# Dilated heads: probabilities divided before the turn and streamed against value pairs on column halves

## The chip, the cores and the metric

One core of a Trainium2 chip runs the whole kernel in one launch. The metric is the device time in microseconds (us) of that core; the median of three runs of the kernel before is 2211.18 us (2210.8 to 2213.64).

## The reference, cut to what matters

The program is three transformer blocks on 512 tokens of width 1024, all in fp32: one block with two other attentions, and then two blocks ("layers" below) whose attention has 16 heads of width 64: four plain heads, four differential heads (two softmaxes each) and eight dilated heads. The change touches the eight dilated heads of both layers. Each dilated head combines three branches by their log-sum-exp, which is the same as one softmax over causal keys with the logarithm of a key's count added to its score:

```python
def dilated_attention(q, k, v, positions):
    ...
    for window, dil in DILATED_PATTERNS:
        o, lse = dilated_branch(q, k, v, window, dil)
        outs.append(o)
        lses.append(lse)
    wts = jax.nn.softmax(jnp.stack(lses, axis=0), axis=0)
    o = jnp.sum(wts[..., None] * jnp.stack(outs, axis=0), axis=0)
    return from_heads(o)
```

Behind it the 16 heads' outputs lie side by side (512 tokens x 1024) and are multiplied by `w_out`.

## The kernel before, in words

Tokens are kept in four tiles of 128. A layer's attention is a list of jobs, `two_jobs`: plain and differential heads alternate, and the eight dilated heads (L0 to L7 below) come last. Class `Plan` (from line 935) writes the order out by hand as steps. Each step has one score tile: 128 queries (tile j) against the 128(j+1) keys that are not in their future; within a dilated head j goes 3, 0, 2, 1. There are 80 score tiles, so steps 0 to 79; the dilated heads' are steps 48 to 79.

For one tile, `attend` does on four engines, in order:

- TensorE multiplies queries by keys into one of three score banks (line 1605); it may not run more than three scores ahead of VectorE's masks.
- VectorE adds the mask and finds the minimum (L2834, with a small read of the result), and ScalarE takes the exponential and the row sum (L2119).
- Three steps later TensorE turns the probabilities 128x128 by 128x128 (transposes, L1631) into one of two banks, and ScalarE copies them out (L2134); for j = 3 VectorE does (L2852).
- Another three steps later TensorE multiplies: a turned 128x128 block of probabilities is the loaded operand and 64 columns of values are streamed (L1617). A dilated head needs 1 + 2 + 3 + 4 = 10 such products. Output: 128 tokens x 64.
- When a head's four tiles are done, VectorE takes the reciprocals of the row sums (L2884) and scales the output into `O2` (`finish`, L2890).

In between, by step numbers in `O2_TURNS`, TensorE turns `O2` back, 128 columns (two heads) by four tiles at a time (`o2_transpose`, L1927), and ScalarE and VectorE split the turned tile into a high and a low part (`o2_high` L2592, `o2_low` L3516). The projection by `w_out` (`slab_features`, lines 1126 to 1128) then runs through four slabs of weights, two of these tiles each; the first slab needs the turned tiles 0 and 1, which are dilated heads 0 to 3. The eighth turned tile is made inside the first slab, behind its bank 2.

In the trace each fp32 matmul is two records, each with its own weight load; a transpose is one.

GpSimd splits weight slabs into high and low parts in slab order (L665, L669, function `run`), as each is loaded and its buffer is free; two of the four `w_out` slabs are split before the dilated heads begin, the third waits until TensorE has used the first.

The differential heads' outputs are normed by a chain at steps 58 to 64 (`DIFF_SQ`, `DIFF_SUM`, `DIFF_ROOT`, `DIFF_SCALE`): ScalarE squares, VectorE sums, ScalarE takes a root (with two table loads), VectorE scales (L2817, L2820). At the start of the attention of the first block, but not here, TensorE is given extra products (`release_clock`) to keep it busy.

Of the kernel before, what the change touches and what calls it, by code (L numbers as in the profile page):

```python
# [221 lines left out]
def build(nc, xT_d, slabs_d, ada_d, c_d, cols_d, rows_d, consts_d, strips_d, pos_d, cpos_d,  # L222
# [5 lines left out]
    with ctx:  # L228
# [140 lines left out]
        O2 = at("O2", 100352, [P, TT, D_MODEL])  # L369
# [4 lines left out]
        sq_2 = at("sq_2", 116736, [P, TT * 4 * HD])  # L374
# [65 lines left out]
        cmp_hidden, hidden_ready = sem("cmp_hidden"), sem("hidden_ready")  # L440
        hidden_turned, hid_copied = sem("hidden_turned"), sem("hid_copied")
        cmp_out, cmp_taken, ck_root, ck_ready = sem("cmp_out"), sem("cmp_taken"), sem("ck_root"), sem("ck_ready")
# [19 lines left out]
        scores_ready, scores_masked, probs_ready = sem("scores_ready"), sem("scores_masked"), sem("probs_ready")  # L462
        probsT_ready, copied_act, copied_dve = sem("probsT_ready"), sem("copied_act"), sem("copied_dve")
# [183 lines left out]

        @block.gpsimd
        def _(pool):
# [205 lines left out]
            def run(n0, n1):  # L855
# [3 lines left out]
                with pool.Fori(n0 // 2, n1 // 2) as i:  # L859
                    for s in (0, 1):  # L860
                        split(s, 2 * i + s, i)
# [5 lines left out]
            for n in [mlp0] + [mlp0 + N_UP + N_DOWN + layer * PER_LAYER + first for layer in range(LAYERS)  # L867
# [5 lines left out]
                for layer, ct in enumerate(COUNTS):  # L873
                    if n == INPUTS[layer].base:
                        at = input_low(INPUTS[layer])
                    if n == ct.up:
# [24 lines left out]


        class Place:


            def __init__(self):
                self.meets = self.slab = self.drain = self.norms = self.bank = 0
                self.tile = self.value = self.map = self.pair = self.acopies = self.dcopies = 0
                self.turn = self.turn_a = self.turn_d = self.part = self.ffn = self.conv = 0
                self.x = self.free = self.pairs = self.roots = self.mixes = self.folds = 0  # L910

        def meeting(name, eng, at_):

            def meet(n=1):
                for _ in range(n):
                    at_.meets += 1
                    eng.drain().then_inc(arrived[name], 1)
                    for other in ("pe", "act", "dve"):
                        eng.wait_ge(arrived[other], at_.meets)
            return meet  # L920

        def slab_view(t, slot, k, n):
            return t[:, slot, 0:k * n].rearrange("p (k n) -> p k n", k=k)

        TURN_LAG, PAIR_LAG, COMBINE_LAG = 3, 5, 2
        S_BANKS, PT_BANKS, O_BANKS = 4, 2, 2
        M_SLOTS, P_SLOTS, PT_SLOTS, P_PAIRS = 2, 4, 3, 8

        FILL = (1, 1, 1, 1, 1)
        FILL_2 = ()

        class Plan:


            def __init__(self, jobs):
                self.scores, self.values, self.sums = [], [], []
                for m, jb in enumerate(jobs):
                    self.sums.append([sum(len(x["q"]) for x in jobs[:m]) + c for c in range(len(jb["q"]))])  # L940
                tiles, m = [], 0
                while m < len(jobs):
                    group = [m + 1, m] if m + 1 < len(jobs) and is_pair(jobs[m + 1]) else [m]
                    for j in (3, 0, 2, 1):
                        for g in group:
# [2733 lines left out]
```

## Time and profile before

| what | value |
|---|---|
| runs | 2213.64, 2210.80, 2211.18 us (median 2211.18) |
| profiled execution, first to last instruction (span) | 2210.5 us |
| what lies around the span | 0.7 us to the median of the runs; the profiled execution has no other time of its own on the page |
| TensorE busy | 2158.2 us, 98% of the span |
| VectorE, ScalarE, GpSimd busy | 1498.9, 946.0, 1195.8 us |
| granted clock of TensorE, mean | 0.996 |

In the profile PE is TensorE's matmuls, PEld its weight loads, DVE VectorE, ACT ScalarE, POOL GpSimd. A record's duration contains its way through the array, so records of a busy PE overlap; what a record costs in a stream is the distance from its start to the next start. A granted clock of 1.0 is 2.4 GHz, of 0.5 is 1.2 GHz.

### The profile page before, as it was taken

Reading aid. Unit: us, or ns where it says so; the run is one execution under the profiler, and the core shown is the slowest. Engines: PE = TensorE matmul, PEld = TensorE weight load, DVE = VectorE, ACT = ScalarE, POOL = GpSimd, SP = SyncE. Lnnn points to the kernel's source line nnn. Section 1 sums busy time; section 2 is a strip of 40 time slices with the busy share of each in tenths; the row PEclk is TensorE's granted clock in tenths of the full one; section 3 lists DMA queues with packets and bytes.
Section 4 is the critical chain, followed back from the end, with each engine's and each line's share of the span. In section 5 each row is a group of like instructions: output and inputs, shape, how many; then the busy total and the mean of one; then the engine's idle time right before and its main releaser. Section 6 shows DMA issues by size and latency. Waiting matters only on the chain.

```text
span 2210.5 us, 33160 instructions
## 1 busy us (share of the span) xinstructions
PE 2158.2 (98%) x12377; PEld 1842.0 (83%) x12377; DVE 1498.9 (68%) x2234; ACT 946.0 (43%) x1891; POOL 1195.8 (54%) x594
## 2 busy tenths in 40 slices
PE   6999999999999999999999999999999999999997
PEld 4788888877899988887887898888897887889886
DVE  6834777554666592897646777677996727777676
ACT  3254663011556510544743555512545725455412
POOL 4747403776477677745016654577653037544675
PEclk9999999999999999999999999999999999999999
DMA  8322102522133233222002222322322002222221
GB/s 323 153 77 89 55 30 84 190 89 96 58 115 107 105 140 133 93 105 86 1 1 95 96 78 113 113 95 79 113 81 75 1 32 84 86 106 115 95 95 57
DMA packets 32776, 206.78 MB, mean 94 GB/s; under 512 B 4080, under 2 KB 4336, under 8 KB 11632
## 3 DMA queue, kind: packets, MB, share of 16 engines
q1 hardware_dynamic: 32192, 200.27, 24.8%
q10 hardware_dynamic: 432, 4.46, 0.5%
q8 instruction: 99, 1.62, 0.3%
q14 instruction: 53, 0.43, 0.1%
HBM read 202.61 MB, written 2.10 MB: 93 GB/s over the span
## 4 chain that ended last, share of the span: by engine, by line
PE 88%; DVE 6%; issue 1%; ACT 1%; DMA 1%; DVEq 1%; POOL 1%; POOLq 0%; SPq 0%; ACTq 0%
PE PS L1126 18%; PE PS L1128 18%; PE PS L1127 18%; PE PS L1605 5%; PE PS L1617 5%; PE PS L1382 3%; PE PS L1381 3%; PE PS L1383 3%; PE PS L1631 3%; PE PS L1457 2%; PE PS L1459 2%; PE PS L1458 2%; PE PS L1256 1%; PE PS L1259 1%; PE PS L1258 1%
## 5 line engine op out<-in xcount | busy, mean ns | idle before, releaser
L665 POOL TENSOR_TENSOR w_hi<-raw,zero_c 128x512 fp32r<-128x512 f32 (+1 forms) x135 | 281.6, 2104 | 545.5 <-PE PS L1128 544.3
L669 POOL TENSOR_TENSOR w_lo<-raw,w_hi 128x512 fp32r<-128x512 f32 (+1 forms) x135 | 365.0, 2723 | 5.8
L1126 PE MATMUL PS<-b_hi,w_hi 128*128 128x512 f32 x512 | 203.1, 397 | 0.9 <-POOL w_lo L888 0.9
L1127 PE MATMUL PS<-b_lo,w_hi 128*128 128x512 f32 x512 | 203.0, 396 | 0.0
L1128 PE MATMUL PS<-b_hi,w_lo 128*128 128x512 f32 x512 | 203.0, 396 | 0.0
L3345 DVE TENSOR_TENSOR b_lo<-a_all,b_hi 128x512 fp32r<-128x512 f32 x44 | 162.6, 3733 | 49.3 <-ACT b_hi L2490 49.3
L1126 PE MATMUL PS<-f_hi,w_hi 128*128 128x512 f32 x448 | 177.6, 397 | 0.7 <-DVE f_lo L2647 0.7
L1128 PE MATMUL PS<-f_hi,w_lo 128*128 128x512 f32 x448 | 177.6, 396 | 0.0
L1127 PE MATMUL PS<-f_lo,w_hi 128*128 128x512 f32 x448 | 177.6, 396 | 0.0
L688 POOL TENSOR_TENSOR w_lo<-raw,w_hi 128x512 fp32r<-128x512 f32 x48 | 70.9, 1477 | 92.9 <-ACT w_hi L2482 92.9
L1126 PEld LDWEIGHTS PS<-b_hi,w_hi 128*128 128x128 f32 x512 | 96.4, 188 | 24.6 <-POOL w_lo L888 1.1
L1128 PEld LDWEIGHTS PS<-b_hi,w_lo 128*128 128x128 f32 x512 | 96.4, 188 | 23.5
L1127 PEld LDWEIGHTS PS<-b_lo,w_hi 128*128 128x128 f32 x512 | 96.4, 188 | 23.5
L1617 PEld LDWEIGHTS PS<-z,ring 128*128 128x128 f32 x640 | 87.0, 191 | 25.7 <-issue 12.2
L1128 PEld LDWEIGHTS PS<-f_hi,w_lo 128*128 128x128 f32 x448 | 84.4, 188 | 20.5
L1126 PEld LDWEIGHTS PS<-f_hi,w_hi 128*128 128x128 f32 x448 | 84.4, 188 | 20.1 <-issue 1.0
L1127 PEld LDWEIGHTS PS<-f_lo,w_hi 128*128 128x128 f32 x448 | 84.4, 188 | 19.1
L2490 ACT ACTIVATE b_hi<-a_all 128x512 fp32r<-128x512 f32 x44 | 25.3, 623 | 171.4 <-PE PS L1128 171.4
L677 POOL TENSOR_TENSOR w_lo<-raw,w_hi 128x2048 fp32r<-128x2048 f32 (+1 forms) x18 | 59.0, 3293 | 62.2 <-ACT w_hi L2342 62.2
L773 POOL TENSOR_TENSOR w_lo<-raw,w_hi 128x512 fp32r<-128x512 f32 x54 | 71.4, 1323 | 38.4 <-ACT w_hi L2380 38.4
L3307 DVE SCALAR_TENSOR_TENSOR aux<-PS,cols,aux 128x511 f32<-128x511 f32 (+1 forms) x112 | 81.0, 741 | 14.7 <-ACT aux L2462 13.5
L1617 PE MATMUL PS<-z,ring 128*128 128x64 f32 x640 | 85.3, 266 | 1.4 <-ACT ring L2134 1.4
(586 smaller groups left out, 6868.7 us busy)
## 6 DMA issues: line engine op xcount, KB each, us to landing
raw<-slabs_dram SPq DMA_DIRECT2D x161, 1024.0 KB, 4.8
aux<-ada_dram SPq DMA_DIRECT2D x18, 512.0 KB, 5.7
ada_first<-ada_dram SPq DMA_DIRECT2D x11, 512.0 KB, 14.1
cmpw<-cmpw_dram ACTq DMA_DIRECT2D x2, 2048.0 KB, 12.7
ada_late<-ada_dram SPq DMA_DIRECT2D x8, 512.0 KB, 3.2
ada_last<-ada_dram SPq DMA_DIRECT2D x8, 512.0 KB, 6.4
xT<-xT_dram SPq DMA_DIRECT2D x1, 2048.0 KB, 9.3
out_dram<-t SPq DMA_DIRECT2D x4, 512.0 KB, 3.2
```

The source lines that it names most:

```text
L665: high = nc.gpsimd.tensor_tensor(w_hi[:, slot, c], raw[:, slot, c], zero[:, 0:c.stop - c.start], ALU.add)
L669: low = nc.gpsimd.tensor_tensor(w_lo[:, slot, c], raw[:, slot, c], w_hi[:, slot, c].bitcast(f32), ALU.subtract)
L688: return nc.gpsimd.tensor_tensor(pair_ring(w_lo, ct, n, what), pair_operand(ct, n, what), pair_ring(w_hi, ct, n, what).bitcast(f32), ALU.s ...
L773: nc.gpsimd.tensor_tensor(ring_slot(w_lo, j), operand(j), ring_slot(w_hi, j).bitcast(f32), ALU.subtract).then_inc(slab_split if name == "A ...
L1126: nc.tensor.matmul(out, a_hi_, b_hi_, start=start, stop=False)
L1127: nc.tensor.matmul(out, a_hi_, b_lo_, start=False, stop=False)
L1128: return nc.tensor.matmul(out, a_lo_, b_hi_, start=False, stop=stop)
L1381: nc.tensor.matmul(out, wh[:, k, :], xh, start=first, stop=False, skip_group_check=True)
L1605: nc.tensor.matmul(PS[:, step % s_banks, 0:128 * nb], query_tile(jobs[m]["q"][c], j), jobs[m]["k"][:, 128 * lo:128 * (lo + nb)], start=Tru ...
L1617: last = nc.tensor.matmul(PS[:, 6 + m % O_BANKS, 64 * j:64 * j + 64], turned_slot(ring, v, 512)[:, 128 * b:128 * b + 128], jobs[m]["v"](lo ...
L3307: V.scalar_tensor_tensor(out=t[:, sh:], in0=src[:, 0:SEQ - sh], scalar=cols[:, w:w + 1], in1=t[:, sh:], op0=ALU.mult, op1=ALU.add)
L3345: V.tensor_tensor(b_lo[:, f, :], a_all[:, f, :], b_hi[:, f, :].bitcast(f32), ALU.subtract).then_inc(b_low_ready, 1)
```

## The change

For the eight dilated heads ("wide" jobs) only:

- The row sum's reciprocal is taken tile by tile on VectorE, two steps behind the score (32 small instructions a layer), and GpSimd multiplies the probabilities by it in place (`normalise`, 32 instructions a layer). On GpSimd's queue this stands behind the first two `w_out` slabs and ahead of the third.
- The turn waits for GpSimd and comes five steps behind the score instead of three; six slots of probabilities instead of four. The copies out of the turn's banks go to a whole-head buffer `wide_pT` (four of them), not to the ring.
- When both heads of a pair are turned, `wide_values` multiplies: 64 columns of values are loaded, and the turned probabilities of one key block, 512, 384, 256 or 128 queries long, are streamed. Head 2i goes to output partitions 0 to 63 and head 2i+1 to 64 to 127 of one bank; the two alternate. The four pairs come at steps 62, 70, 78 and, for the last, inside the first `w_out` slab behind its bank 0.
- The result lies turned already, so `O2` keeps only the plain and differential heads, the dilated heads' `finish` and four of the eight `o2_transpose` go, and `o2_high`/`o2_low` read the pair's bank.
- The first `w_out` slab takes its banks in order 0 to 7; three semaphores of another stage become one; buffers move.

```diff
+        TURN_LAG, PAIR_LAG, COMBINE_LAG = 3, 5, 2
+        WIDE_LAG, WIDE_INV_LAG, WIDE_VALUE_LAG = 5, 2, 2
...
                 for t in tiles:
-                    due[t] = t[2] + TURN_LAG
+                    due[t] = t[2] + (TURN_LAG if jobs[t[0]]["wide"] is None else WIDE_LAG)
...
-                    self.pvs.setdefault(turn + 2, []).append(v)
-                    self.takes.setdefault(turn + 3, []).append(v)
-                self.steps = turn + 4
+                    if not self.is_wide[v]:
+                        self.pvs.setdefault(turn + 2, []).append(v)
+                        self.takes.setdefault(turn + 3, []).append(v)
+                self.steps = turn + (1 if self.is_wide[-1] else 4)
+                self.wide_step = {pair: at_step[vs[-1]] + WIDE_VALUE_LAG for pair, vs in self.pair_values.items()}
...
-        O2_TURNS = [(56, 4, 3), (59, 5, 7), (63, 0, 10), (67, 6, 8), (70, 7, 8), (73, 1, 12), (80, 2, 14)]
+        O2_TURNS = sorted([(56, 4, 3), (59, 5, 7), (67, 6, 8), (72, 7, 8)] + [(wide_at[pair], pair, None) for pair in range(4)])
...
+            def normalise(layer):
+                plan = Plan(two_jobs)
+                for w, i in enumerate(plan.wide_scores):
+                    m, _, j, _ = plan.scores[i]
+                    _, nb = key_range(two_jobs[m], j)
+                    probs = probs_slot((ring_2, ring_x, ring_y), plan.slots[i], 128 * nb)
+                    pool.wait_ge(wide_inv_ready, len(plan.wide_scores) * layer + w + 1)
+                    nc.gpsimd.tensor_scalar(probs, probs, wide_inv[:, w % 8:w % 8 + 1], None, ALU.mult
+                                            ).then_inc(wide_normed, 1)
...
                         if is_pair(jobs[m]):
                             pe.wait_ge(combined, joined[v])
+                        elif plan.is_wide[v]:
+                            pe.wait_ge(wide_normed, w0 + plan.wide_scores.index(i) + 1)
...
+            def wide_values(pair, copied):
+                for ready in (copied_act, copied_dve):
+                    pe.wait_ge(ready, max(count for s_, count in copied if s_ is ready))
+                for b in range(TT):
+                    for g in (0, 1):
+                        h = 2 * pair + g
+                        last = nc.tensor.matmul(PS[64 * g:64 * g + 64, 6 + pair % 2, 128 * b:512],
+                                                z2[:, 5, b, 64 * h:64 * h + 64], wide_pT[h % 4][:, b, 128 * b:512],
+                                                start=b == 0, stop=b == TT - 1, skip_group_check=True)
+                last.then_inc(turned, 1)
...
+                    if step - WIDE_INV_LAG in plan.wide_scores:
+                        i = step - WIDE_INV_LAG
+                        w, (m, _, j, _) = plan.wide_scores.index(i), plan.scores[i]
+                        dve.wait_ge(probs_ready, g0 + i + 1)
+                        if w >= 8:
+                            dve.wait_ge(wide_normed, at_.wide + w - 7)
+                        V.reciprocal(wide_inv[:, w % 8:w % 8 + 1], rowsum[:, plan.sums[m][0] % 8, j:j + 1]
+                                     ).then_inc(wide_inv_ready, 1)
...
                 def last_turn(b):
-                    if b == 2:
+                    if b == 0:
                         o2_transpose(KD - 1)
...
-                              bank_ready=o2_banks, order=(0, 1, 2, 4, 5, 6, 7, 3), after=last_turn)
+                              bank_ready=o2_banks, order=range(KD), after=last_turn)
```

## Rows read from the trace of the kernel before

**Rows 1.** The page, part 1: busy time and share of the span:

```profile
PE 2158.2 (98%) x12377; PEld 1842.0 (83%) x12377; DVE 1498.9 (68%) x2234; ACT 946.0 (43%) x1891; POOL 1195.8 (54%) x594
```

**Rows 2.** Windows: the dilated stretch of layer 1, of layer 2, layer 2's end:

```profile
core 0: us, PE busy (x) PEld busy (x) DVE busy (x) ACT busy (x) POOL busy (x), PEclk, DMA share, GB/s
1087.76:1139.63 51.87, 50.42 (x372) 43.27 (x371) 35.05 (x108) 36.17 (x108) 0.00 (x0) 1.00 0.01 1
1735.00:1787.00 52.00, 50.54 (x370) 43.29 (x370) 35.92 (x113) 36.85 (x112) 0.00 (x0) 1.00 0.00 1
1783.00:1789.00 6.00, 6.00 (x55) 5.95 (x55) 2.62 (x9) 3.30 (x10) 0.00 (x0) 1.00 0.00 0
```

**Rows 3.** Timeline of PE, head L3: start, length, line, records:

```profile
1105.54 1.02 PE L1605 MATMUL PS<-T2a,T 128*128 128x512 f32 x2
1106.40 0.78 PE L1617 MATMUL PS<-z,ring 128*128 128x64 f32 x6
...
1108.08 0.81 PE L1605 MATMUL PS<-T2a,T 128*128 128x384 f32 x2
1108.73 1.00 PE L1617 MATMUL PS<-z,ring 128*128 128x64 f32 x8
1109.57 0.39 PE L1631 MATMUL PS<-consts,ring 128*128 128x128 f32 x2
1109.80 0.60 PE L1605 MATMUL PS<-T2a,T 128*128 128x256 f32 x2
1110.23 0.33 PE L1617 MATMUL PS<-z,ring 128*128 128x64 f32 x2
1110.40 0.61 PE L1631 MATMUL PS<-consts,ring 128*128 128x128 f32 x4
1110.84 0.60 PE L1927 MATMUL PS<-consts,O 128*128 128x128 f32 x4
```

**Rows 4.** Groups of DVE and ACT in 1092 to 1132 us:

```profile
L2834 DVE CUSTOM_DVE_ANT_0 ring<-PS,strip 128x256 f32<-128x256 f32 x7 | 3.0, 423 | 3.9 <-PE PS L1605 3.9
L2852 DVE COPY ring<-PS 128x512 f32<-128x512 f32 x7 | 4.8, 691 | 3.4 <-PE PS L1617 1.7 <-PE PS L1631 1.7
L3516 DVE TENSOR_TENSOR o_lo<-PS,o_hi 128x512 fp32r<-128x512 f32 x6 | 4.1, 688 | 0.4 <-ACT o_hi L2592 0.2
L2884 DVE RECIPROCAL stats<-rowsum 128x4 f32<-128x4 f32 x7 | 1.2, 175 | 0.2
L2890 DVE TENSOR_TENSOR O<-PS,stats 128x256 f32<-128x256 f32 x7 | 3.0, 425 | 0.5
...
L2119 ACT ACTIVATE ring<-ring,negmax 128x256 f32<-128x256 f32 x7 | 3.5, 502 | 0.3 <-DVE negmax L2834 0.3
L2592 ACT ACTIVATE o_hi<-PS 128x512 fp32r<-128x512 f32 x6 | 3.5, 584 | 0.0
```

**Rows 5.** Groups of POOL, all of the span:

```profile
L665 POOL TENSOR_TENSOR w_hi<-raw,zero_c 128x224 fp32r<-128x224 f32 x2 | 1.1, 558 | 0.0
L786 POOL TENSOR_TENSOR w_hi<-raw,zero_c 128x512 fp32r<-128x512 f32 x8 | 8.2, 1041 | 21.9 <-DMA raw<-slabs_dram 21.7 <-issue 0.2
L783 POOL TENSOR_TENSOR w_lo<-raw,w_hi 128x512 fp32r<-128x512 f32 x8 | 10.3, 1290 | 0.4 <-issue 0.4
```

**Rows 6.** DVE with two operands in SBUF: POOL idle, and the page's:

```profile
L2820 DVE TENSOR_TENSOR O<-O,rows 128x1024 f32<-128x1024 f32 x1 | 1.2, 1226 | 0.1
...
L3345 DVE TENSOR_TENSOR b_lo<-a_all,b_hi 128x512 fp32r<-128x512 f32 x44 | 162.6, 3733 | 49.3 <-ACT b_hi L2490 49.3
```

**Rows 7.** Windows in the first block's attention:

```profile
225.00:228.00 3.00, 1.49 (x11) 1.36 (x12) 1.21 (x5) 2.97 (x9) 2.15 (x2) 1.00 0.00 0
228.00:231.00 3.00, 3.00 (x13) 2.40 (x12) 1.26 (x3) 1.59 (x6) 3.00 (x3) 0.50 0.01 3
```

More of the change, by code:

```diff
@@ L645, in _, with __init__ @@
             sp.wait_ge(stored, 16 * KD // 2)
+        class Place:
+            def __init__(self):
+                self.meets = self.slab = self.drain = self.norms = self.bank = 0
+                self.tile = self.value = self.map = self.pair = self.acopies = self.dcopies = 0
+                self.turn = self.turn_a = self.turn_d = self.part = self.ffn = self.conv = 0
+                self.x = self.free = self.pairs = self.roots = self.mixes = self.folds = 0
+                self.narrow = self.wide = 0
@@ new lines, in turned_slot, with on_vector, key_range, job @@
+        def turned_slot(ring, u, n):
+            return ring[0][:, M_SLOTS + P_SLOTS + u % PT_SLOTS, 0:n]
+        def on_vector(jb, j):
+            return j == TT - 1 and jb["vector"]
+        def key_range(job, j):
+            lo = max(0, j - 2) if job["window"] else 0
+            return lo, j - lo + 1
+        def job(q, k, v, out, strip=None, window=False, coef=None, mode="set", turned_by=None, vector=True, wide=None):
+            return dict(wide=wide, vector=vector, q=q if isinstance(q, tuple) else (q,), k=k, v=v, out=out, strip=strip, window=window, coef=coef, mode=mode, turned_by=turned_by)
@@ new lines, in apart, with laid, turned_counts @@
+        def apart(n, src, slots, masks):
+            parts = [(slots[i], masks[:, i:i + 1]) for i in range(masks.shape[1])]
+            return (src, P, parts, []) if n % 2 == 0 else (src, P, [], parts)
+        def laid(bank, dst):
+            return bank.rearrange("p (t d) -> p t d", t=TT) if len(dst.shape) == 3 else bank
+        def turned_counts(items):
+            out, a, d = [], 0, 0
+            for _, _, acts, dves in items:
+                a, d = a + len(acts), d + len(dves)
+                out.append((a, d))
+            return out
@@ new lines, in build, with turn_split @@
+        two_turns += [apart(i, two_src(3, 128 * i), dilated_q[2 * i:2 * i + 2], halves) for i in range(4)]
+        two_turns += [whole(i, two_src(4, 128 * i), P, T2a[:, i, :], 1.0) for i in range(4)]
+        two_turn_chunk = [2] * 2 + [0] * 2 + [1] * 2 + [0] * 2 + [3] * 4 + [4] * 4
+        HEAD = 8
+        turn_step = {step: HEAD + n for n, step in enumerate((3, 8, 13, 18, 23, 28, 33, 38))}
+        def turn_split(src, hi, lo, n, gains=None):
+            return [(lambda tt, i=i: src(tt, i), hi[:, i, :], lo[:, i, :], gains[i] if gains else None)
+                    for i in range(n)]
@@ L900, in _ @@
                     pool.drain()
[L903 to L920, printed above, removed]
@@ L1590, in attend @@
                         copies.append((copied_act, a))
+                return copies, a, d
+            def attend(jobs, ring, s_banks=S_BANKS, banks_ready=None, also=None, fill=FILL):
+                plan = Plan(jobs)
+                g0, v0, m0, p0 = at_.tile, at_.value, at_.map, at_.pair
+                w0 = at_.wide
+                (copies, a, d), joined = value_copies(jobs, plan), []
+                for m, j, _ in plan.values:
                     at_.pair += is_pair(jobs[m])
@@ L1940, in _ @@
                 at_.turn_d += KD
[L1941 removed]
+                order = o2_order
                 def o2_banks(b):
```

416 lines of the change are left out of this document (219 added, 197 removed).

## The prediction

> **What bounds the kernel now.** The page comes first: TensorE is busy 98% of the span [rows 1], so what ends last is its stream nearly everywhere, and an edit is worth what it takes out of that stream less the idle time it puts in. Next the windows: the stretch from the first dilated score to the first product of the projection lasts 51.9 us in layer 1 and 52.0 in layer 2, with TensorE idle 1.45 us in each, all at full clock; the last 6 us have no idle at all [rows 2]. VectorE and ScalarE are busy 35 and 36 us of the 52, GpSimd not at all. Then the timeline, where the price of a record is the distance to the next start [rows 3]: a score of 512, 384 or 256 columns costs 0.86, 0.65 or 0.43 us, so 0.22 for 128 and 2.16 for a head's four; eight records of the value product take 0.84 us (0.105 each), four of a transpose 0.44 (0.11). A value record streams 64 columns, by the score's rate 0.054 us: it costs twice that, as much as a transpose, so its 128-column load sets it.
>
> Sums go against the span of 2210.5 us; what lies around it (0.7 to the median) is left alone, so a difference is taken from the median, 2211.18. About 0.2%, 4.4 us, is what a measurement of this kernel tells from no change.
>
> **Part 1: TensorE's stream, per layer.** Removed: 8 heads x 10 products x 2 records x 0.105 = 16.8 us, and 4 x 4 turns of O2 x 0.11 = 1.8; together 18.6. Added: per pair 4 key blocks x 2 heads x 2 records, of 512, 384, 256 and 128 columns; loads of 64 columns hide behind streams at least that long. Nothing in this trace uses half of the array's columns, so the price is bounded. Above: every record at the score's price, 2 x 2.16 = 4.3 us a pair, 17.3 a layer, net 1.3 saved. Below: the heads of a pair wholly beside each other, 8.6, net 10.0 saved. They use different columns of the array and different output partitions and alternate in the code, so I take them to run side by side, but starting in order: a head's second record waits for its first, so the pair runs as nine slots, 3 x 0.43 + 2 x 0.325 + 2 x 0.215 + 2 x 0.11 = 2.6 us, 10.4 a layer, net **8.2 saved**. The nearest rows (whole-array records, never two at once [rows 3]) are the upper end; I set it apart as a rival.
>
> The Trainium skill, "TensorEngine Tiling (Array Packing)", Key Properties, states that tiles execute in parallel, but also that changing the tiling mode drains the engine; no run here shows either yet. By the first the stream is the 8.2 saved, by the whole-array rows 1.3.
>
> Going from whole to half columns and back happens eight times a layer. Bound: nothing, or the way through the array that a stream hides, 0.33 less two times 0.105, so 0.12 us [rows 3], 1.0 a layer. I take **0.6**.
>
> **Part 2: the last tile has no cover.** Before, value products fill TensorE while the last tiles are masked, exponentiated and turned, hence the full last 6 us. After, behind the last score (step 79) only 15 transposes remain, 1.65 us. The chain from that score, with rows' durations [rows 4]: mask 0.42, exponential 0.50 (1.0 with hand-overs); ScalarE copies a turned tile of 384 columns (about 0.4, an estimate from the 0.58 of a like operation over 512) and takes the high part of pair 2 (0.58): 2.0; VectorE, in order, takes that low part (0.69) ahead of the last reciprocal (0.18): 2.85; then it copies the turned 512-wide tile (0.69), whose bank the second last turn needs: 3.5; GpSimd divides meanwhile; the two last turns follow (0.55): 4.1. So 4.1 - 1.65 = **2.4 us idle** a layer (2.1 to 2.8). The last pair's product then comes behind bank 0, by when its copies are done, and its high and low parts (1.3 us) hide behind banks 1 to 6.
>
> **Part 3: the clock.** In the first block TensorE was busy 1.49 of 3.0 us and the next 3 us were granted 0.5 [rows 7]; it loses half of those, 1.5 us. The tail is busy 1.65 of 4.1. Nothing or 1.7 us; I take **1.0** a layer.
>
> **Part 4: GpSimd.** The dividing has one tensor and one number a row. Rows [rows 5]: 0.56 us for 224 columns and 1.04 for 512, where one operand is a repeated zero, so 1.68 ns a column and 0.18 fixed: 1280 columns and four instructions make 2.9 us a head. With two full operands (1.29 for 512) at most 3.5. TensorE's pace will be 2.16 + 1.1 (ten turns) + 1.3 = 4.5 a head, so GpSimd keeps up. On its queue the dividing stands behind two splits that end before the stretch (POOL is idle throughout it [rows 2]) and ahead of the third, which waits for TensorE's first slab as before: nothing. SP's queue is not passed by anything.
>
> Latency: a turn comes five steps behind its score, but the reciprocal sits behind the mask two steps on. For a 512-wide tile: 1.5 us to the third score's end, 0.7 to its mask's end, 0.18, then 1.04, 3.4 us with hand-overs; TensorE's five steps hold 3.7 without a product in them. The margin is 0.3, so some turns wait: nothing to 1.5, I take **0.4** a layer, since each pair's product lets the others catch up.
>
> **Part 5: VectorE and ScalarE.** VectorE loses eight finishes (0.175 + 0.425) and gains 32 reciprocals at no more than 0.175: 35.1 - 4.8 + 5.6 = 35.9 us; ScalarE stays at 36 [rows 2, 4]. TensorE's stream in the stretch falls to about 40. The cover over these two goes from 14 to 4 us, and their work is not even: until step 61 no product fills TensorE, while VectorE finishes the differential heads. There I put 1.0 us (0 to 2). Around steps 62 to 67 the norm of the differential heads blocks first ScalarE, then VectorE, and turned tile 6 waits for it; less of the product's stream covers it than before, and its two passes over 1024 columns read two operands in SBUF (1.23 us alone) while GpSimd now works; such an operation took 3.73 us for 512 columns where GpSimd was splitting weights [rows 6]. There 0.8 (0 to 2.5). Together **1.8**.
>
> On the last point the Trainium skill, "SBUF — State Buffer", section "SBUF: two separate sides", says that GpSimd and a VectorE instruction with two SBUF inputs lock each other out for a whole instruction. By it each pass waits for one division at most, which lies inside that bound.
>
> **Sum** per layer: -8.2 + 0.6 + 2.4 + 1.0 + 0.4 + 1.8 = -2.0, two layers -4.0: 2211.2 - 4.0 = **2207 us**. With every bound of parts 2 to 5 at its end: from 2199 (-8.2 + 2.1 = -6.1 a layer; 2195 with the lower end of part 1) to 2218 (-8.2 + 2.8 + 1.7 + 1.0 + 1.5 + 4.5 = 3.3). The other edits move buffers and semaphores, at nothing: each wait on the merged semaphore names the same event, and the slab's new bank order waits for tiles that are ready by then.
>
> **Rivals.**
> 1. *One half behind the other: slower.* If records on half the columns queue like the others, the stream saves 1.3, while the tail still costs 2.4, clock 1.0, mode 0.6. Longer products give the others more time, so waits are 1.2 in place of 2.2. Per layer +3.9: **2219**, 2213 to 2222. For it: every pair of matmul records in the trace follows one another. Against: disjoint columns and partitions. The point that decides is a pair's product at about 3.2 us (18.6 less what parts 2 to 5 cost, by four); above, no gain is left.
> 2. *Side by side, and the others keep up.* Only the tail and mode changes cost: -8.2 + 2.4 + 0.6 = -5.2 a layer: **2201**, 2196 to 2204. For it: VectorE and ScalarE are idle 16 us of the stretch now, much of it waiting for TensorE. Against: their work bunches at the norm.
> 3. *GpSimd sets the pace.* From 4.5 us a head on it decides; at twice the two-operand price, 7.0, it adds 20 us a layer less the waits it covers: about **2243**. Against: no row of POOL is near that price per column.
>
> The change could also fail to do what it says only by rival 1's route; the removed records are certain.
>
> **Chances.** Forecast 0.40, rival 1 0.33, rival 2 0.22, rival 3 0.05. Faster than 2206.8: 0.17 of the forecast's 0.40, since its number, 2207, stands on that bound (its own range is 2199 to 2218), and rival 2: 0.39. Within 0.2%: 0.19 of the forecast and 0.07 of rival 1: 0.26. Slower than 2215.6: 0.04 of the forecast, 0.26 of rival 1, rival 3: 0.35. The likeliest case gives 2207. Cases of both signs hold most of the chance, so the range runs from rival 2's end, 2196, to rival 1's, 2222; it leaves out rival 3 and the tails, under 2 in 10.
>
> **What would show it.** Part 1: the pair's products as 16 records with 64 loaded columns, 2.6 us from first to next start if side by side, 4.3 if not; whether two records of different halves start together. Part 2: idle of some 2.4 us between the last score and the first projection product, released by VectorE's copy or GpSimd. Part 3: a window at 0.5 behind it. Part 4: the new POOL group at about 1.0 us for 512 columns. Part 5: idle of TensorE before scores, released by the mask, at the norm's place. The prediction is wrong if the stretch changes by more than 8 us, or if TensorE waits for GpSimd at most turns.

## The result, and the profile after

The changed kernel takes 2219.89 us (median of 6 runs, 2218.94 to 2222.52) against 2212.11 for the kernel before on the same chip: ratio 1.0037, 95% interval 1.0026 to 1.0049. It is slower by 0.37%. The prediction said 2207 and faster; its range, to 2222, held the time. The profiled execution took 2222.52 us, the longest of the six, and its mean granted clock is the lowest, 0.993 against 0.995 and 0.996 in the other five, so what is read from it is at the upper end, the price of the clock above all. The page's first line, which answers to [rows 1]:

```profile
PE 2153.6 (97%) x12153; PEld 1815.0 (82%) x12153; DVE 1493.7 (67%) x2266; ACT 946.2 (43%) x1891; POOL 1267.8 (57%) x658
```

Windows of the changed kernel: the stretch from the first dilated score to the first product of the projection in layers 1 and 2, then two pieces of layer 1, behind the norm and behind the tail:

```profile
core 0: us, PE busy (x) PEld busy (x) DVE busy (x) ACT busy (x) POOL busy (x), PEclk, DMA share, GB/s
1085.66:1140.03 54.37, 44.80 (x248) 28.84 (x247) 33.41 (x126) 35.37 (x107) 34.41 (x32) 0.94 0.00 1
1740.91:1795.23 54.32, 44.75 (x249) 28.80 (x247) 33.56 (x126) 35.29 (x107) 34.40 (x32) 0.94 0.00 1
1112.50:1119.30 6.80, 6.00 (x18) 3.45 (x17) 3.97 (x13) 2.84 (x11) 3.07 (x3) 0.50 0.00 0
1139.80:1143.20 3.40, 3.40 (x11) 2.33 (x12) 0.00 (x0) 0.86 (x2) 0.00 (x0) 0.50 0.00 0
```

The same two stretches of the kernel before, here from the start of the first dilated score, as in the windows above ([rows 2] have layer 1's from a little earlier and a rounded window of layer 2):

```profile
1087.81:1139.63 51.82, 50.37 (x372) 43.22 (x371) 34.99 (x108) 36.12 (x108) 0.00 (x0) 1.00 0.01 1
1736.92:1788.74 51.82, 50.36 (x372) 43.22 (x371) 34.99 (x108) 36.13 (x108) 0.00 (x0) 1.00 0.00 1
```

From the start of one layer's stretch to the next it is 1740.91 - 1085.66 = 655.25 us, where before it was 1736.92 - 1087.81 = 649.11: 6.1 us a layer. The stretch was 51.82, with TensorE busy 50.37. Now it is 54.37, with TensorE busy 44.80, and idle 9.57 in place of 1.45. Of the busy time 3.0 us are the price of half clock: in the 6.8 us of the third window TensorE is busy 6.0, and a score of 512 columns takes 1.71 us to the next start there, where it took 0.86 [rows 3]. So the stretch is 5.57 + 3.0 = 8.6 us shorter in work, 8.1 longer in idle time, and 3.0 longer by the clock. Behind it stand the last pair's product (2.4), a turn of `O2` less (0.4), and another 3.4 us at half clock (fourth window, 1.7 lost). In all per layer: work -6.6, idle time +8.1, clock +4.7, sum +6.2, and 6.1 is what the starts show. (The spans differ by 10.2 us and not by two times 6.1, as the stretch of layer 1 starts 2.15 us earlier than before; its start lies anywhere from 1084.1 to 1088.7 us in the runs below.)

TensorE's timeline at the first pair's product (start, length, line, records; `128*64` is the loaded operand):

```profile
1104.96 0.30 PE L1681 MATMUL PS<-consts,ring 128*128 128x128 f32 x1 [0.16 <-ACT T L2206]
1105.19 0.64 PE L1700 MATMUL PS<-wide_pT,z 128*64 128x512 f32 x1
1105.20 0.64 PE L1700 MATMUL PS<-T,z 128*64 128x512 f32 x1
1105.67 0.59 PE L1700 MATMUL PS<-wide_pT,z 128*64 128x512 f32 x1
...
1107.29 0.27 PE L1700 MATMUL PS<-wide_pT,z 128*64 128x128 f32 x1
1107.49 0.70 PE L1653 MATMUL PS<-T2a,T 128*128 128x256 f32 x2
```

Two records of different heads start 10 ns apart: the halves work side by side. From the first start to the next score it is 2.30 us, where a pair's sixteen records would cost 4.3 at the price of records on the whole array [rows 3].

What TensorE's matmuls waited for in layer 1's stretch, and under it what its weight loads waited for (us in total, times, longest). No score (L1653) is among the matmuls that waited; all are turns, and what they waited for are copies and low parts:

```profile
PE PS L1681 <- ACT T L2206: 3.4, 4, 1.7
PE PS L1999 <- DVE o_lo L3608: 2.8, 2, 1.4
PE PS L1681 <- DVE wide_pT L2938: 1.6, 2, 0.8
PE PS L1681 <- ACT ring L2211: 1.2, 1, 1.2
```

```profile
PEld PS L1681 <- issue: 8.7, 14, 1.6
PEld PS L1681 <- POOL ring L1045: 4.8, 5, 1.8
PEld PS L1681 <- POOL ring_y L1045: 2.0, 3, 1.3
```

GpSimd's groups in the same stretch (count, busy us and mean ns, idle before):

```profile
L1045 POOL TENSOR_SCALAR ring<-ring,stats 128x512 f32<-128x512 f32 x5 | 7.8, 1565 | 52.1 <-DVE stats L2923 52.1
L1045 POOL TENSOR_SCALAR ring<-ring,stats 128x384 f32<-128x384 f32 x6 | 7.5, 1246 | 3.8 <-DVE stats L2923 3.8
L1045 POOL TENSOR_SCALAR ring<-ring,stats 128x256 f32<-128x256 f32 x6 | 5.5, 925 | 3.6 <-DVE stats L2923 3.6
L1045 POOL TENSOR_SCALAR ring<-ring,stats 128x128 f32<-128x128 f32 x5 | 3.0, 604 | 0.9 <-DVE stats L2923 0.9
```

A head's four divisions take 1.565 + 1.246 + 0.925 + 0.604 = 4.34 us. The two operands' rows [rows 5] had given at most 3.5.

VectorE and ScalarE beside the product of 1105.19 to 1107.49, and TensorE ahead of it and behind it:

```profile
1106.27 0.55 DVE L2912 CUSTOM_DVE_ANT_0 ring<-PS,strip 128x384 f32<-128x384 f32 x1
...
1108.23 0.42 DVE L2912 CUSTOM_DVE_ANT_0 ring<-PS,strip 128x256 f32<-128x256 f32 x1 [1.33 <-PE PS L1653]
```

```profile
1106.86 0.61 ACT L2191 ACTIVATE ring<-ring,negmax 128x384 f32<-128x384 f32 x1 [1.18 <-DVE negmax L2912]
...
1107.59 1.28 ACT L2678 ACT_TABLE_LOAD   x1
...
1109.37 1.28 ACT L2191 ACT_TABLE_LOAD   x1
```

```profile
1101.47 0.63 PE L1999 MATMUL PS<-consts,O 128*128 128x128 f32 x4 [1.39 <-DVE o_lo L3608]
...
1103.99 0.81 PE L1653 MATMUL PS<-T2a,T 128*128 128x384 f32 x2
...
1111.79 0.63 PE L1681 MATMUL PS<-consts,ring 128*128 128x128 f32 x4 [1.66 <-ACT T L2206]
...
1126.87 0.63 PE L1999 MATMUL PS<-consts,O 128*128 128x128 f32 x4 [1.43 <-DVE o_lo L3608]
```

While the product runs, TensorE makes no score, and VectorE runs dry for 1.33 us. ScalarE's 1.18 us are another matter: the score of 384 columns that it waits for was begun at 1103.99, ahead of the product, but VectorE, behind with the norm's sum, a copy and a low part, masked it at 1106.27 only. Behind the product both are late: ScalarE loads its tables for the norm's root and back, two times 1.28 us, with the copy behind them, and TensorE waits 1.66 us for that copy and is at half clock from 1112.5 on. The kernel before has the same two loads. VectorE's and ScalarE's busy time, 33.4 and 35.4 us, is no more than before [rows 2].

### The profile page after: what moved, and what is told of

Its sections match the earlier page's. It is cut to its first block, busy times and chain, and to the rows that moved or that the text cites. A ratio compares the mean times of both kernels' runs of the same rounds, so it can differ in the third digit from the quotient of the medians.

```text
span 2220.7 us, 32738 instructions
## 1 busy us (share of the span) xinstructions
PE 2153.6 (97%) x12153; PEld 1815.0 (82%) x12153; DVE 1493.7 (67%) x2266; ACT 946.2 (43%) x1891; POOL 1267.8 (57%) x658
## 4 chain that ended last, share of the span: by engine, by line
PE 83%; DVE 8%; issue 2%; DMA 2%; ACT 1%; DVEq 1%; POOL 1%; POOLq 1%; SPq 0%; ACTq 0%
PE PS L1167 18%; PE PS L1169 18%; PE PS L1168 18%; PE PS L1653 5%; PE PS L1665 3%; PE PS L1422 3%; PE PS L1424 3%; PE PS L1423 3%; PE PS L1681 2%; PE PS L1498 2%; PE PS L1500 2%; PE PS L1499 2%; DMA raw<-slabs_dram 1%; PE PS L1700 1%; DVE PS L3525 1%
## 5 line engine op out<-in xcount | busy, mean ns | idle before, releaser
L1045 POOL TENSOR_SCALAR ring<-ring,stats 128x384 f32<-128x384 f32 (+3 forms) x44 | 47.3, 1085 | 120.9 <-DVE stats L2923 120.9
L972 POOL TENSOR_TENSOR w_lo<-raw,w_hi 128x1024 fp32r<-128x1024 f32 x24 | 66.0, 2766 | 28.3 <-DVE aux L3535 20.2
```

## The experiments

All were timed in five rounds beside the kernel before; a ratio is to that kernel on the same chip, with its 95% interval. The changed kernel stands at 1.0037.

**1. The division left out.** The reciprocals stay, the division goes:

```diff
-                        normalise(layer)
...
-                            pe.wait_ge(wide_normed, w0 + plan.wide_scores.index(i) + 1)
+                            pe.wait_ge(probs_ready, g0 + i + 1)
...
```

> Leaves out the division of the dilated heads' probabilities (the reciprocals are still taken); a turn waits for the exponential itself. Theory (the chain through GpSimd sets TensorE's waits: TensorE's loads wait 6.8 us a layer for GpSimd's divisions, and idle time brings half clock): most of those waits go, the stretch from the first dilated score to the projection falls from 54.4 to about 49 to 50 us a layer and the time from 2220 to about 2210. Rival A (the work of VectorE and ScalarE, placed at fixed steps, sets the waits): the waits move to the masks and copies, at most 2 us gained, 2218. Rival B (half clock after the tail and the norm is the whole loss): 2217 to 2218, since both places of idle stay.

Measured: 2218.76 us, ratio 1.0031 (1.0022 to 1.0040). The first theory fell. The table of waits had put 6.8 us a layer on GpSimd; with GpSimd gone the same loads wait for the exponential, and the matmuls' waits stand where they were (stretch of layer 1, lines shifted by one):

```profile
PE PS L1680 <- ACT T L2205: 3.4, 4, 1.7
PE PS L1998 <- DVE o_lo L3605: 2.8, 2, 1.4
```

```profile
PEld PS L1680 <- ACT ring L2190: 8.1, 8, 1.8
PEld PS L1680 <- ACT ring_y L2190: 1.5, 2, 0.9
```

So a wait that stands on a weight load is not by itself a cost to the matmuls.

**2. One column divided.** `tensor_scalar` on `probs[:, 0:1]`, the hand-overs as they were.

> GpSimd divides one column in place of 128 to 512 (the rest of the division is left out), so that its two hand-overs stay and its 4.3 us a head shrink to an estimated 1.1 (4 x 0.28, the fixed part of the line through 0.604 and 1.565 us). Theory that the price per column was mis-sized: the time comes within 2 us of the kernel without the division. If the hand-overs from VectorE to GpSimd to TensorE cost as much as the work: half way between that kernel and the changed one, about 2215. Rivals A and B as there: 2217 to 2218.

Measured: 2217.80, 1.0031 (1.0022 to 1.0041), the same as without: neither GpSimd's work nor its hand-overs held most of the time.

**3. The heads one behind the other.** In `wide_values` the loop over the two heads goes outside the one over key blocks.

```diff
-                for b in range(TT):
-                    for g in (0, 1):
+                for g in (0, 1):
+                    for b in range(TT):
```

> The changed kernel, but a pair's product takes the four records of one head and then those of the other, in place of head by head in turn. Theory: the two heads then share nothing, the pair's product goes from 2.30 to about 4.3 us, and as other engines catch up meanwhile some of the 8 us a layer is covered: 5 to 7 us a layer more, 2230 to 2234. If the sharing is worth nothing here because TensorE waits anyway: 2220 to 2222.

Measured: 2236.12, 1.0110 (1.0095 to 1.0126). The first pair's product:

```profile
1105.56 1.93 PE L1700 MATMUL PS<-wide_pT,z 128*64 128x512 f32 x5
1107.12 0.64 PE L1700 MATMUL PS<-T,z 128*64 128x512 f32 x1
...
1108.02 1.46 PE L1700 MATMUL PS<-T,z 128*64 128x384 f32 x6
1109.41 0.70 PE L1653 MATMUL PS<-T2a,T 128*128 128x256 f32 x2
```

It takes 3.85 us in place of 2.30 (the last records of one head still run beside the first of the other). Four times 1.55 are 6.2 us a layer, and the time is 8.1 a layer longer. TensorE's idle time in the stretch is 10.7 us in its trace, where the changed kernel has 9.6: the longer product covered nothing. That speaks against any cover by the product.

**4. Waits for the own bank only, one turn later.**

```diff
-(59, 5, 7)
+(61, 5, 7)
...
-                    pe.wait_ge(turned_dve, base + n)
+                    pe.wait_ge(turned_dve, base + max([m + 1 for m in range(n) if O2_TURNS[m][1] >= 4], default=0))
```

> Turns of the differential tiles wait only for the earlier tile of their own PSUM bank (the third no longer for the low part of the second pair), and the second of them stands two steps later, 61 in place of 59. Theory: two waits of 1.4 us a layer go, 2.8 a layer, and half of it is taken up by the next wait: 2215 to 2217 (2214.3 if all of it stays). Rival A (other engines set the pace in this stretch): the wait appears at the next score or turn, 2219 to 2220.

Measured: 2219.11, 1.0035 (1.0021 to 1.0049). The two waits of 1.4 us for VectorE's low parts went and the next ones grew (1.72 us for ScalarE's copy, 1.97 for VectorE's behind the norm), as rival A had it.

**5. The products spread.** One key block a step, over four steps; own banks as in 4.

```diff
+        wide_block = {wide_at[pair] + b: (pair, b) for pair in range(3) for b in range(TT)}
...
+                    if step in wide_block:
+                        o2_transpose(o2_order.index(wide_block[step][0]), [wide_block[step][1]])
```

> The products of the first three pairs are taken one key block a step over four steps, in place of four blocks at one step; the differential tiles wait for their own bank only. After the first four runs the theory is: TensorE is idle 8.5 us a layer at fixed places, with or without the division, because a pair's product is one lump that covers nothing elsewhere, where before the value products lay evenly between the scores. By it the idle time falls to 3 to 5 us a layer, the stretch from 54.4 to about 49 to 50 us, and with a little for twelve more changes of mode a layer the time is 2210 to 2213. Rival C (VectorE's and ScalarE's work at the norm of the differential heads sets the waits, wherever the products lie): the waits before step 66 stay and 2217 to 2219 is measured.

Measured: 2214.77, 1.0014 (1.0005 to 1.0023). Three fifths of the loss go; no half clock is left in the stretch, 51.16 us long, and TensorE is idle 6.7 us of it in place of 9.6. The pieces cost more than the lump: 1.01, 0.79, 0.58 and 0.37 us from first start to next score, 2.75 against 2.30.

**6. The norm's passes left out.** VectorE's two passes that scale the differential heads are left out.

> Leaves out VectorE's two passes over the differential heads that apply the norm and its gain (2 x 1.23 us a layer); the squares, the sums and the root stay. Rival C (the norm sets the waits): the idle 1.66 and 0.80 us behind it and the 3.4 us lost at half clock after it go, 5 us a layer, 2210. The lump theory: the 2.5 us at most, part of it taken up by the waits next to it, 1 to 2.5 a layer, 2215 to 2218.

Measured: 2216.11, 1.0022 (1.0013 to 1.0031): 1.9 us a layer for 2.5 us of VectorE's work, and not all of what was lost. In its trace the wait of 0.80 us behind the passes goes and that of 1.66 stays; idle time falls by 0.5 us a layer only, and the time at half clock from 10.2 to 3.4 us.

**7. ScalarE's copies ahead of its exponential**, where a step turns dilated tiles alone: the loop over `plan.turns` moved up in ScalarE's `attend`.

> ScalarE copies the turned tile of a step ahead of that step's exponential in place of behind it. If TensorE's waits for ScalarE's copies (4.6 us in the stretch of layer 1: 3.4 for earlier copies' slots and banks and 1.2 for a differential one) come from the copy's place behind an exponential that waits for VectorE's mask, they go and some of the half clock with them: 3 to 5 us a layer, 2210 to 2214. If the copies are late because VectorE and ScalarE as a whole are late there, the wait turns up at the masks: 2218 to 2221.

Measured: 2215.81, 1.0022 (1.0013 to 1.0031), two fifths of what was lost, though nothing is computed less. Its trace does not show where the gain lies: in place of the waits of 1.66 and 0.80 us stand three of 0.56, 1.39 and 1.58, the idle time is 9.6 us a layer as in the changed kernel, and the half clock, 3.4 us a layer in place of 10.2, is that of one execution, for the runs' mean clocks (0.994 to 0.996) are no higher than the changed kernel's.

**8. The third pair's product two steps later**, `self.wide_step[2] += 2`.

> The third pair's product is taken two steps later, at step 80, behind the last score, where TensorE is idle 1.08 and 0.81 us while the last head is divided, turned and copied, and falls to half clock. If the product covers that idle time: 1.9 a layer and 1.7 us of half clock go, 3.6 a layer, 2212 to 2214. If the place only moves the waits (the idle shows up between steps 78 and 80, or the copies of the last tiles are late by as much): 2218 to 2221.

Measured: 2217.11, 1.0029 (1.0019 to 1.0039): less than expected, and the interval reaches the changed kernel's. The tail's wait of 1.08 us went, one of 0.78 came before it, and the last (0.77) stayed.

**9. Products that nobody reads, where TensorE is idle.**

```diff
-        FILL_2 = ()
+        FILL_2 = {65: 2, 67: 1, 81: 1, 83: 1}
...
```

> The changed kernel with products that nobody reads (128x512, bank 7) put into TensorE's stream ahead of the turns it waits for: two at step 65, one each at steps 67, 81 and 83, where the trace shows 1.66, 0.80, 1.08 and 0.81 us of idle time. They shorten no wait; by the score's row each is 0.86 us, so at most 0.4 a layer is added to what was idle. Theory: the half clock comes from this idle time, and by the profiled run it costs 5.1 us a layer (6.83 and 3.41 us at half); kept busy, TensorE stays at full clock, 2 to 5 us a layer, 2211 to 2216. If the half clock is not brought by the idle time there, or most runs have little of it: 2219 to 2221.

Measured: 2216.67, 1.0023 (1.0014 to 1.0032). Layers 1 and 2:

```profile
1088.54:1141.18 52.64, 46.35 (x259) 28.72 (x257) 33.33 (x126) 35.24 (x106) 34.37 (x32) 1.00 0.00 1
1740.38:1793.04 52.66, 46.34 (x258) 28.72 (x257) 33.46 (x126) 35.25 (x106) 34.37 (x32) 1.00 0.00 1
```

Though TensorE has 4.3 us more to do, the stretch is 1.7 shorter than the changed kernel's, at full clock throughout. The granted clock is 0.996 or 0.997 in all eleven runs, where the changed kernel's six have 0.993 to 0.996: with the idle places filled the clock stays up. The time falls by 3.2 of the 8 us that were lost, with fillers that have a price too; the two intervals overlap. But idle time does not bring half clock each time. Run 2 has the same wait of 1.66 us in layer 1, 10.2 us of idle time, and full clock in the whole stretch:

```profile
1086.34:1138.68 52.34, 42.15 (x248) 27.41 (x247) 33.05 (x126) 35.28 (x106) 9.04 (x32) 1.00 0.00 1
```

**10. Spread and copies first together**, with the second differential tile's turn at 61 (5, 7 and 4 in one).

> The products spread over four steps (as in the run with spread products), ScalarE's copies ahead of its exponentials, the second differential tile at step 61, own banks. If the three gains are of one kind (idle time that each takes from the same places) little is added to the spread's: 2213 to 2215. If they add (5.1 and 4.1 and 0.8 below the changed kernel): 2210 to 2211, level with the kernel before.

Measured: 2209.03, 0.9992 (0.9983 to 1.0001). The gains add, and idle time is down to 5.7 us a layer.

**11. Two pieces in place of four.**

> As the run before this, but each of the three products in two pieces of two key blocks, two steps apart, the third tile's turn a step later. In the spread run the four pieces took 1.01, 0.79, 0.58 and 0.37 us, 2.75 in place of 2.30, and the records ahead of a piece are longer too; half the changes of mode save about 0.3 to 0.6 us a pair, 1 to 2 a layer. If that is so and the pieces are still small enough to cover: 2 to 3 us below the run in four pieces, 2208 to 2211. If the lump is what matters: above it, 2213 to 2216.

Measured: 2209.76, 0.9993 (0.9984 to 1.0002): no difference from four in time. The traces show why: with six pieces in place of twelve TensorE's work in layer 1 is 41.6 us where 10 has 43.4, so a piece costs 0.29 us, and idle time is 6.7 us where 10 has 5.7.

**12. As 10, the division left out.**

> As the run with spread products and copies first, with the division left out. In the changed kernel leaving it out gave 1 us, since the waits had other causes as well; with those smaller, GpSimd's chain may be next: its waits in the spread run are 0.5 and 0.7 us a layer. If so 2 to 3 us below the same kernel with the division; if VectorE and ScalarE still set the waits, within 1 us of it.

Measured: 2208.54, 0.9987 (0.9978 to 0.9996), within 1 us of 10.

**13. All mended but the lump**: copies first, own banks, turns at 61, 69 and 74, the norm's passes at steps 64 and 66.

> Everything of the best version but the spread: the products stay lumps at one step; ScalarE copies first, own banks, the differential tiles' turns at steps 61, 69 and 74, and the norm's two passes on VectorE two steps apart (64 and 66). Tells the lump from the rest: if the lump is the cause of its own (VectorE and ScalarE run dry while it lasts, and TensorE waits behind it), 2214 to 2217, some 5 above the same version spread out. If copies, turns and norm alone were at fault: 2210 or less, level with the spread version.

Measured: 2212.05, 0.9997 (0.9988 to 1.0006). The lump kept, the loss of time is gone, but not the idle time (8.5 us in layer 1, windows under 14).

**14. As 13, the products spread.**

> The version with spread products and copies first (2209.0), with the norm's two passes over the differential heads taken at steps 64 and 66 in place of one behind the other. TensorE's longest idle time in it is 2.20 us, for VectorE's copy of a turned tile behind those passes. If the passes in a row are its cause, half of it goes, 1 us a layer and a little of half clock: 2206 to 2208, clear of the kernel before. If VectorE is late there as a whole: 2208.5 to 2209.5.

Measured: 2210.15, 0.9995 (0.9986 to 1.0004), and no better than 10. In time the spread is worth no more beside the mended order than the intervals hold. Layer 1's stretch in 13 and in 14:

```profile
1084.91:1134.50 49.59, 41.07 (x249) 27.28 (x247) 33.02 (x126) 35.56 (x106) 35.27 (x32) 1.00 0.00 1
1086.78:1135.29 48.51, 43.44 (x249) 26.75 (x247) 33.05 (x126) 36.33 (x107) 35.40 (x32) 1.00 0.00 1
```

The lumps hold 8.5 us of idle time, the pieces 5.1; but nine pieces more cost TensorE 2.4 us (0.26 each), and that takes most of the gain. So the lump is a cause of idle time of its own. The longest wait of 10 (2.20 us for VectorE's copy behind the norm's passes) fell to 0.54, and a new one of 1.38 for GpSimd came 3 us later. TensorE, VectorE and GpSimd there:

```profile
1113.58 0.52 PE L1682 MATMUL PS<-consts,ring 128*128 128x128 f32 x3 [0.54 <-DVE wide_pT L2953]
...
1116.78 0.44 PE L1682 MATMUL PS<-consts,ring_y 128*128 128x128 f32 x2 [1.38 <-POOL ring_y L1046]
```

```profile
1111.33 1.23 DVE L3636 TENSOR_TENSOR O<-O,stats 128x1024 f32<-128x1024 f32 x1
...
1114.07 1.23 DVE L3641 TENSOR_TENSOR O<-O,rows 128x1024 f32<-128x1024 f32 x1
```

```profile
1110.65 1.25 POOL L1046 TENSOR_SCALAR ring<-ring,stats 128x384 f32<-128x384 f32 x1 [1.95 <-DVE stats L2938]
1112.94 0.93 POOL L1046 TENSOR_SCALAR ring<-ring,stats 128x256 f32<-128x256 f32 x1 [1.04 <-DVE stats L2938]
1114.07 3.24 POOL L1046 TENSOR_SCALAR ring_y<-ring_y,stats 128x512 f32<-128x512 f32 x2 [0.21 <-DVE stats L2938]
```

```profile
L1046 POOL TENSOR_SCALAR ring_y<-ring_y,stats x20: 602/1087/2654, 1095.6 to 1779.9; 128x512 f32<-128x512 f32 x6, 128x128 f32<-128x128 f32 x6, 128x384 f32<-128x384 f32 x4, 128x256 f32<-128x256 f32 x4
```

The division that starts with VectorE's pass at 1114.07 takes 2654 ns at most in this run, where others of 512 columns take 1565: GpSimd stood still for most of the pass. By the Trainium skill, "SBUF — State Buffer", section "SBUF: two separate sides", a VectorE instruction with two SBUF inputs and GpSimd lock each other out for a whole instruction; the trace agrees for this division, with 1.09 us here, and disagrees for the one before it: VectorE's pass of 1111.33 started in the midst of a division of 384 columns (1110.65 to 1111.90), and neither took longer than elsewhere (1.23 and 1.25 us). In the changed kernel it is the same with the first pass, and no division starts while a pass runs, so nothing of it showed there.

**15. The norm three steps later** (61, 63, 65, 67, 69).

> As the run before this, with the norm's steps later by three (squares 61, sums 63, root 65, passes 67 and 69), so that all of it lies beside the pieces of the first two products, and the turns that need it at 72 and 76. If what costs is that VectorE's and ScalarE's extra work lies where no product covers it: the 1.49 us of idle time at step 57 to 59 goes too, 2 to 3 us a layer in all, 2203 to 2206. If it only moves the wait: 2206 to 2209.

Measured: 2209.60, 0.9993 (0.9984 to 1.0002): the waits only moved (idle time 5.2 us a layer, 5.1 in 14).

**16. All copies of the stretch ahead of the exponentials.**

> The version with the products spread and the norm's passes apart (2210.2), with ScalarE's copies ahead of the exponential at every step of the dilated stretch (before, at steps where both kinds of heads are turned, they stood behind it), and the third differential tile at step 75. TensorE's first two waits in it are 1.23 and 1.49 us for copies that stood behind an exponential waiting for VectorE's mask. If the order on ScalarE is the cause, they shrink by 1 to 2 us a layer: 2206 to 2208. If VectorE, which masks late while it finishes the last narrow heads, is the cause: 2209 to 2210.5.

Measured: 2207.19, 0.9984 (0.9975 to 0.9993). The first wait, 1.23 us, went; the second, 1.50, stayed. Idle time is 4.3 us a layer.

**17. As 16, six steps from score to turn.**

```diff
-        WIDE_LAG, WIDE_INV_LAG, WIDE_VALUE_LAG = 5, 2, 2
+        WIDE_LAG, WIDE_INV_LAG, WIDE_VALUE_LAG = 6, 2, 2
```

> As the run before this, with a turn six steps behind its score in place of five (the same six slots). TensorE waits 1.38 us for GpSimd's division in the version with the norm's passes apart, because the reciprocal stands behind a pass of the norm on VectorE. If the chain score, mask, exponential, reciprocal, division is what then ends last, one step more (about 1.1 us) takes 1 to 2 us a layer: 2 to 4 below the run before this. If the copies end last: no difference, or up to 1 us longer at the end of the stretch.

Measured: 2201.67 (5 runs, 2200.63 to 2201.88), 0.9953 (0.9940 to 0.9967). It beats the kernel before by 0.47%. Its edits to the changed kernel, all told: products spread (5), own banks and turns at 61, 69 and 75 (4), copies first (7, 16), the norm's passes at 64 and 66 (14), lag six. Layers 1 and 2:

```profile
1084.14:1129.56 45.42, 43.16 (x248) 26.66 (x247) 32.25 (x125) 35.75 (x106) 34.90 (x32) 1.00 0.00 1
1729.57:1775.00 45.43, 43.17 (x248) 26.67 (x247) 32.35 (x125) 35.67 (x106) 34.87 (x32) 1.00 0.01 1
```

Idle time is 2.3 us a layer, against 9.6 in the changed kernel and 1.45 before, at full clock. Against 16 the wait of 1.50 us for ScalarE's copy has gone, those for GpSimd fell from 2.2 to 0.5 us, and one of 1.30 for VectorE's copy behind the norm's passes has come.

**18. As 17, the norm later.**

> As the run before this, with the norm's steps later by three, the turns that need it at 72 and 76. With the copies first and the lag longer, what is left of VectorE's bunch at the norm lies beside the products: 0 to 2 us below the run before this; 2204 to 2207 if all three causes are independent.

Measured: 2201.46, 0.9953 (0.9940 to 0.9967), the same.

## Why the prediction was wrong

**The stream (part 1) was right in its mechanism.** The heads run side by side, as taken; the pair's product is 2.30 us where nine slots gave 2.6. The net of TensorE's work is -6.6 a layer, where -7.6 was said with the changes of mode, though the products alone would have made it 1.2 better; what the rest of the stream lost by it was not told apart. A change is not free: with more pieces TensorE's work grows by 0.26 to 0.29 us for each (10 and 11, 13 and 14). The Trainium skill, "TensorEngine Tiling (Array Packing)", Key Properties, says both that tiles run in parallel and that a change of mode drains the engine; the traces agree on the first, with 10 ns between the starts, and for the second they show this price, not the drain itself. Rival 1 is refuted; 3 shows what it would have looked like.

**The tail (part 2)** was taken at 2.4 us of idle time and is 1.08 + 0.81 = 1.9, released by ScalarE's and VectorE's copies.

**GpSimd (part 4)** was mis-sized in price, 4.34 us a head for 2.9 (at most 3.5), yet its effect of 0.4 us a layer stands: leaving it out gave about 0.5 (1.1 us in all, inside the intervals). The sentence that the prediction fails "if TensorE waits for GpSimd at most turns" named a sign that says nothing: the loads waited, and nothing hung on it.

**VectorE and ScalarE (part 5) is the step that failed.** It said 1.8 us a layer, at most 4.5. The idle time of 8.1 more than before, less 1.9 at the tail and 0.5 for GpSimd, leaves 5.7. Both of its places are beyond their bounds: ahead of the first product TensorE's waits come to 2.8 us (taken at 1.0, at most 2), between it and the last score to 4.5 (taken at 0.8, at most 2.5), the 1.45 us of before included. The sign that it named, idle time ahead of scores, released by the mask, did not come: TensorE waits ahead of turns, for copies and low parts. VectorE's two passes, whose bound allowed for GpSimd in their way, took 1.23 us each, as alone.

The working weighed 36 us of their work against 40 of TensorE's stream and took what was between as cover. But cover counts step by step. Before, value products stood between the scores of every step, and an engine that was late had a few tenths each time; the change took these away at every step and gave back three lumps. The traces bear this out. With lumps TensorE is idle 9.6 us a layer, with the products spread 6.7 (5); with the order mended 8.5 and, in layer 2, 7.6 with lumps (13), and 5.1 spread (14). What the order adds beyond the spread is 0.6 to 1.0 us at each step (copies first, 10; the norm's passes apart, 14; all copies first, 16) and 2.0 for a turn six steps behind its score (17). These are two remedies that take different waits. That 13 costs no more time than the kernel before does not mean that its waits are gone: its idle time eats what the stream saves, and its trace has little half clock (none in layer 1, 3.4 us in layer 2). No run left out the norm's root with its two table loads, which stand right ahead of the 1.66 us, so its part is open. All that the same stretch of the kernel before shows of the kind is

```profile
PE PS L1631 <- ACT ring L2134: 1.4, 3, 0.6
```

where the value products of every step stood ahead of the turns.

**The clock (part 3)** was said to cost 1.0 us a layer, at most 1.7, for one tail (the 1.7 are half of the 3.41 us that the clock stays low in the trace of before, from 228.02 us on; [rows 7] shows 3 of them). In the profiled execution the tail costs 1.7, and the idle time behind the norm, which the term left out, another 3.0. That execution has more of it than most: the other five runs were granted a higher clock, run 2 shows the same waits at full clock, and filling the idle places gave 1.6 us a layer (9).

So in the profiled execution the sum failed by +3.9 in part 5 and +3.7 in part 3, which hangs on part 5, and by +1.0 in part 1; the other terms are off by 0.5 or less. The median run is 7.8 us behind the kernel before, 3.9 a layer; how that divides between idle time and clock was not measured. **Rival 2**, that the others keep up, gave 2201 us. The change itself does not do that, but run 17, which computes the same with the products spread, the others' order altered and one more step of lag, is at 2201.7: the change's saving is there, and what it lacked was an even stream and an order that let the others keep up. How much of run 17's last 5.5 us is the chain through GpSimd and how much the lateness of VectorE and ScalarE ahead of it was not told apart, and 17 without the spread was not tried.

## What to carry to other kernels

When work is taken out of the engine that bounds the kernel, ask step by step what stood beside that work, not what the sums of busy time leave over: an even stream covers others' hand-overs, a lump of the same length does not. Before giving such a change up, spread the lump and move the others' waiting instructions (copies ahead of work that waits, one more step of lag in the same buffers): here this made 0.37% slower into 0.47% faster. Look at the idle time beside the total: two runs of the same time (13 and 14) had 8.5 and 5.1 us of it. A wait that a table shows on a weight load is not yet a cost; take its cause away and see whether the matmul still waits.

## What was not expected of the hardware

GpSimd's product of one tensor with one number a row, in place, costs 2.5 ns a column and 0.28 us fixed (0.604 us for 128 columns, 1.565 for 512), more than the row of two tensors gave (1.29 us for 512, [rows 5]). It stood still for 1.09 us when a division started together with a VectorE pass over two operands, and not at all when the pass started in the midst of a division (14); in 15 such a pass, 0.27 us behind a division's start, took 1.39 us in place of 1.23. A piece of the half-column product between other work costs 0.26 to 0.29 us more than in a lump. Half clock came in the midst of busy stretches, behind an idle time of 1.66 us that ended at 1111.79, and lasted 6.8 us, while idle times of 1.39 and 1.43 us that ended at 1101.47 and 1126.87 brought none. The length of the wait does not decide it: 1.66 us brought none in layer 1 of run 2, and 2.20 us none in run 10. [rows 7] had shown 3 us of half clock behind a half-empty start.
